# Per-head sums of squares and the spread of their scales: 32x32 turns on VectorE in place of PE transposes

## The reference

```python
y = concatenate([sb_out, fx_out, m_out])          # (1, 1024, 20 * 64)
yf = y.reshape(b, s, TOTAL_HEADS, HEAD_DIM)
yf = yf * rsqrt(mean(yf * yf, axis=-1) + EPS)     # per token and head, EPS = 1e-6
yf = yf.reshape(b, s, MIX_WIDTH) * out_norm_w
x = x + (yf * silu(gate)) @ w_out
return rmsnorm(x, final_norm_w)
```

## Time and profile before

| | |
|---|---|
| runs, device time | 803.50, 803.75, 803.94 us, median 803.75 |
| span of the profiled execution | 801.8 us |
| PE, DVE, ACT, POOL busy | 792.6, 580.4, 454.9, 239.2 us |
| share of the span | 99%, 72%, 57%, 30% |
| transfers | 88.9 MB, mean 111 GB/s |

### The profile page before, as it was taken

One profiled execution on the slowest core, in us unless ns is written; L12 is line 12 of the kernel. 1 busy time (PEld: TensorE's weight loads), 2 busy tenths in 40 slices (PEclk: granted clock), 3 DMA queues, 4 the chain that ended last, 5 costly groups with the idle time before them and its releaser, 6 DMA issues.

```text
span 801.8 us, 12113 instructions
## 1 busy us (share of the span) xinstructions
PE 792.6 (99%) x4184; PEld 671.3 (84%) x4184; DVE 580.4 (72%) x1178; ACT 454.9 (57%) x928; POOL 239.2 (30%) x378
## 2 busy tenths in 40 slices
PE   9999999999999999999999999999999999999997
PEld 8878888888888888888888888888888888888885
DVE  6877666676668887767788776779657677875575
ACT  7767665556647555665745576565546483542232
POOL 0112631342245225234533341454233111410000
PEclk9999999999999999999999999999999999999999
DMA  9414823114122411411061131104312298152532
GB/s 345 155 53 151 273 80 117 54 41 131 40 79 51 134 40 67 132 39 54 30 175 46 67 103 69 53 27 114 110 54 67 82 371 300 54 179 79 184 132 105
DMA packets 35276, 88.93 MB, mean 111 GB/s; under 512 B 3592, under 2 KB 11784, under 8 KB 34192
## 3 DMA queue, kind: packets, MB, share of 16 engines
q1 hardware_dynamic: 35216, 88.17, 33.3%
HBM read 57.72 MB, written 21.53 MB: 99 GB/s over the span
## 4 chain that ended last, share of the span: by engine, by line
PE 94%; DVE 2%; DMA 2%; issue 1%; ACT 1%; SPq 0%; ACTq 0%; DVEq 0%
PE banks L818 16%; PE banks L820 16%; PE banks L819 16%; PE banks L863 11%; PE banks L993 9%; PE banks L1013 5%; PE banks L980 5%; PE banks L1012 5%; PE banks L979 5%; PE banks L1064 1%; PE banks L950 1%; PE banks L945 1%; PE banks L1033 1%; DMA hT<-wo_dram 1%; PE banks L935 1%
## 5 line engine op out<-in xcount | busy, mean ns | idle before, releaser
L818 PE MATMUL banks<-hT,w_parts 128*128 128x512 f32 x576 | 237.3, 412 | 0.2 <-DVE sb_heads L1661 0.2
L820 PE MATMUL banks<-hT,w_parts 128*128 128x512 f32 x576 | 225.9, 392 | 0.0
L819 PE MATMUL banks<-hT,w_parts 128*128 128x512 f32 x576 | 225.4, 391 | 0.0
L1775 DVE TENSOR_TENSOR pT<-banks,pT 128x512 fp32r<-128x512 f32 x208 | 108.3, 563 | 88.9 <-ACT pT L1222 87.3
L1222 ACT ACTIVATE pT<-banks 128x512 fp32r<-128x512 f32 x208 | 92.5, 497 | 135.3 <-PE banks L993 135.1
L820 PEld LDWEIGHTS banks<-hT,w_parts 128*128 128x128 f32 x576 | 108.1, 188 | 24.5
L818 PEld LDWEIGHTS banks<-hT,w_parts 128*128 128x128 f32 x576 | 108.5, 188 | 15.0 <-DVE sb_heads L1661 0.7
L819 PEld LDWEIGHTS banks<-hT,w_parts 128*128 128x128 f32 x576 | 108.9, 189 | 13.3
L1490 POOL TENSOR_TENSOR w_parts<-w_raw,w_parts 128x1024 fp32r<-128x1024 f32 x34 | 81.5, 2398 | 95.9 <-ACT w_parts L1122 95.9
L1735 DVE TENSOR_TENSOR_SCAN work<-work 128x639 f32<-128x639 f32 (+3 forms) x64 | 90.6, 1416 | 4.7 <-POOL work L1497 4.6
L1198 ACT ACTIVATE work<-banks 128x512 f32<-128x512 f32 (+2 forms) x96 | 47.5, 495 | 71.0 <-PE banks L980 60.8
(11 more groups left out here) (248 smaller groups left out, 1366.3 us busy)
## 6 DMA issues: line engine op xcount, KB each, us to landing
w_raw<-in_w_tiles SPq DMA_DIRECT2D x36, 512.0 KB, 4.1
hT<-wo_dram SPq DMA_DIRECT2D x14, 512.0 KB, 8.0
fx_heads<-fx_heads SPq DMA_DIRECT2D x8, 512.0 KB, 7.5
negL<-negL_dram SPq DMA_DIRECT2D x8, 512.0 KB, 6.5
yT_dram<-silu SPq DMA_DIRECT2D x8, 512.0 KB, 5.1
sb_heads<-sb_heads SPq DMA_DIRECT2D x8, 512.0 KB, 7.0
negL<-yT_dram SPq DMA_DIRECT2D x8, 512.0 KB, 5.0
work<-in_x SPq DMA_DIRECT2D x6, 512.0 KB, 7.0
```

What stands on the lines that cost most here:

```text
L818: pe.matmul(o, w[0][:, k, :], hT[:, 0, k, tok], start=(k == 0), stop=False)
L819: pe.matmul(o, w[0][:, k, :], hT[:, 1, k, tok], start=False, stop=False)
L820: mm = pe.matmul(o, w[1][:, k, :], hT[:, 0, k, tok], start=False, stop=(k == KT - 1))
L1775: dve.tensor_tensor(pT[:, n % 3, 1, cols], banks[:, T_BANK + n % 2, cols], pT[:, n % 3, 0, cols].bitcast(F32), ALU.subtract).then_inc(t_lo, 1)
```

## The change

**N1.** ACT squares `yT` out of SBUF straight into the small bank, with the factor 1/64 in its scale. It is feature-major there, and DVE turns it in 32x32 blocks: within each block rows and columns change places, but the blocks stay where they are. Into `o_tmp` go 128 partitions x 512, in which partition 32 i + t holds token t of a 32-column block, and the 32 columns of a block are a quarter of the features of the pair. DVE sums 32 at a time to 16 numbers of a half. A head has two quarters, so its sum is that of two partition groups: at the second N1 of a phase DVE copies `head_sums` with neighbouring groups of 32 partitions swapped, in four copies, and adds. The scales are then 128x32 for a phase where they were 128x16, with each number there twice, and DVE's start, POOL's Newton steps and ACT's spread work on that shape.

**NT.** For the softmax heads EPS times the square of the row totals must come in the same layout. In the six phases behind such a pair POOL copies the totals four times side by side at tick 1 (`totals`), a new small piece NT at tick 2 transposes that with one PE transpose, and DVE turns it by 32x32 blocks and makes `head_eps` in two instructions.

**N3.** DVE turns the spread scales of one half from SBUF into the small bank, and goes on as before.

**Waits.** N1 and N3 are no longer in PE's row. ACT's square waits for `small_done` and `o_read`; DVE's N3 waits for `spread`. `o_tmp` is used twice now, so ACT's copy of an output waits for the N1 before it. ACT's sigmoids of a phase's first ticks wait for N3's `small_done`. SP's row is not changed.

```diff
@@ small_pieces @@
+            if c and PHASES[ph - 1][0] != "sb":
+                out.append(Small("NT", 0, ph - 1, UNITS * ph + TOTALS_TICK + 1))
@@ PE: small(n) @@
-                if n:
+                if n and p.what in ("VT", "MT", "NT"):
                     pe.wait_ge(small_done, n)
...
-                elif p.what == "N1":
-
-                    pe.wait_ge(o_read, 4 * p.of + 2 + TURN[p.c] + 1)
-                    for b in range(4):
-                        t = 4 * p.c + b
-                        mm = pe.transpose(o[:, b * P:(b + 1) * P], yT[:, t * P:(t + 1) * P], ident[:, :])
+                elif p.what == "NT":
+                    pe.wait_ge(totals_in, NT_BEFORE[n] + 1)
+                    mm = pe.transpose(o[:, 0:P], totals[:, :, :].rearrange("p i f -> p (i f)"), ident[:, :])
                 else:
-                    pe.wait_ge(spread, p.of + 1 + (TURN[p.c] if p.of == LAST else 0))
-                    for b in range(4):
-                        t = 4 * p.c + b
-                        mm = pe.transpose(o[:, b * P:(b + 1) * P], spread_of(p.of)[:, t * P:(t + 1) * P], ident[:, :])
+
+                    return
...
-            small(small_of("N3", 0, LAST))
@@ ACT: square_rows, spread_scales, output_lo @@
+                if g % 4 == 3:
+
+                    act.wait_ge(small_done, small_of("N1", 1, t.ph) + 1)
+                elif g % 4 == 0 and g:
+                    act.wait_ge(small_done, small_of("N1", 0, t.ph - 1) + 1)
...
-                act.wait_ge(small_ready, n + 1)
-                act.activation(banks[:, SMALL_BANK, :], banks[:, SMALL_BANK, :], ACT.Square).then_inc(sq_done, 1)
+                p = SMALL[n]
+                act.wait_ge(small_done, n)
+                act.wait_ge(o_read, 4 * p.of + 2 + TURN[p.c] + 1)
+                act.activation(banks[:, SMALL_BANK, :], yT[:, p.c * CW:(p.c + 1) * CW], ACT.Square, scale=HD ** -0.5).then_inc(sq_done, 1)
...
-               head3[:, 0, NB * c0:NB * c1].unsqueeze(2).broadcast_to((P, NB * (c1 - c0), HD)),
+               head3[:, 0, 2 * NB * c0:2 * NB * c1].unsqueeze(2).broadcast_to((P, 2 * NB * (c1 - c0), Q4)),
@@ POOL: spread_totals @@
+                row = rowsum[:, ph % 2, :, :].rearrange("p b h -> p (b h)")
+                pool.tensor_copy(totals[:, :, 0:2 * NB], row.unsqueeze(1).broadcast_to((P, P // Q4, 2 * NB))).then_inc(totals_in, 1)
@@ DVE: small pieces @@
+                elif p.what == "NT":
+
+                    dve.wait_ge(small_ready, READY_BEFORE[n] + 1)
+                    link(dve.transpose(totals[:, :, :].rearrange("p i f -> p (i f)"), src[:, 0:P]))
+                    for h in range(2):
+                        mine = slice(h * HD, (h + 1) * HD)
+                        z = totals[mine, :, h:2 * NB:2].rearrange("p a b -> p b a")
+                        ins = dve.scalar_tensor_tensor(out=head_eps[mine, :].rearrange("p (b a) -> p b a", b=NB), in0=z, scalar=EPS, in1=z,
+                                                       op0=ALU.mult, op1=ALU.mult)
+                    ins.then_inc(small_done, 1)
                 elif p.what == "N1":
...
-                    link(dve.reduce_sum(sums, src.rearrange("p (n d) -> p n d", d=HD), AX_X))
+                    link(dve.transpose(o_tmp[:, :], src))
+                    ins = dve.reduce_sum(head_sums[:, mine], o_tmp[:, :].rearrange("p (n d) -> p n d", d=Q4), AX_X)
...
+                    for i in range(P // Q4):
+                        ins = dve.tensor_copy(head_swap[i * Q4:(i + 1) * Q4, mine], head_sums[(i ^ 1) * Q4:(i ^ 1) * Q4 + Q4, mine])
+                    link(ins)
...
                 else:
-                    dve.wait_ge(small_ready, n + 1)
+                    dve.wait_ge(spread, p.of + 1 + (TURN[p.c] if p.of == LAST else 0))
+                    link(dve.transpose(src, spread_of(p.of)[:, cols]))
                     dve.wait_ge(gy_done, 2 * p.of + TURN[p.c] + 1)
```

51 lines of the change are left out of this document (37 added, 14 removed).

## The result

The changed kernel takes 822.72 us (median of four runs, 821.22 to 823.79), the kernel before 803.62: ratio 1.0236, 95% interval 1.0222 to 1.0251. Slower was the likelier side, but the time lies 11.7 us above the forecast of 811.0 and 2.7 above the end of the range.

The account below looks back on a forecast made before the run. PE, 99% busy, and DVE together bound the stick-breaking stretch. Memory -0.3, forgetting -1.6, stick-breaking +8.8 and +1.4, end -1.1 sum to +7.2 us on 803.75: 811.0 us, range 797 to 820.

Parts of the forecast that it names:

- The price of N1: DVE's turn, four copies and additions at a phase's second N1: 1.2 us later, 0.9 to 2.0.
- POOL: Three Newton steps on 128x32 instead of 128x16: 0.42 us longer, 0 to 0.7.
- The path: Stick-breaking phase: N1 with POOL +1.6, first N3 +0.72, holding PE at Q's evacuation +2.3 us; phase sum +2.9.
- the second N3: Stick-breaking phase, between the two evacuations: +0.72 less 0.25 slack, +0.5 us.
- The forgetting phases behind: Two forgetting phases following stick-breaking ones: +0.85 us each, +1.7 together.
- The second memory phase: Memory phase where DVE and ACT alternate closely: -0.3 us taken of its -1.65.
- The last phase and the end: Last stick-breaking phase +1.4 us; the end -1.1, four blocks and idle saved against one uncovered N1.
- The full gain: Rival: PE's waits at DVE move with PE and turns fit DVE's idle; 786.5 us, chance 0.12.
- the second: Rival: only the back-to-back stretch pays, copies and POOL's part fit waits, forgetting phases keep their gain; 800 us, chance 0.18.
- the dear turns: Rival: DVE turns cost two passes, 1.22 us each; 820.6 us, chance 0.12.
- the point of decision: Full-gain rival's threshold: 2.2 us of DVE work between 385 and 407; less is free, more is paid.
- The cheap ends: Turn 0.48, POOL +0, copies 0.08: stick-breaking phase 1.1 us less, forgetting one 0.9; total 804.7 us.

Follow-up runs that it names:

- d_split: Kernel before, none of the change, DVE given one idle 1.2 us reduction at each of the two N3 in three stick-breaking phases; 810.23 us.
- n3_turn: Kernel before with only N3's turns moved to DVE, N1 left on PE's transposes; 805.40 us, ratio 1.0026.
- n1_turn: Changed kernel with N3 put back on PE's transposes, N1 still turned by DVE; 814.92 us, ratio 1.0145.
- after_pool: Changed kernel with the second N1 at tick 6 and POOL's Newton steps in tick 7 behind its masks; 799.93 us, ratio 0.9962.
- best_b: after_pool with first forgetting phase's second N1 at tick 7, second N3 from tick 11 to 12, first memory pair's spread and N3 a tick earlier; 794.69 us.
- d_long: Kernel before, none of the change, DVE given three idle 1.22 us reductions at the first N3 of three stick-breaking phases; 820.28 us.
- d_warm: d_long with fourteen zero-weight matmuls on PE ahead of its wait in each of the three phases; 814.36 us.
- after_early: Changed kernel with the second N1 of a phase at tick 6 in place of 7; 816.99 us, ratio 1.0170.
- after_p8: Changed kernel, second N1 still at tick 7, POOL's Newton steps behind the masks of tick 8, spread and N3 one tick later; 814.72 us.

## Why the forecast was wrong

- *The bound.* Right. PE and DVE share it in the stick-breaking phases; PE's saved time was waited away at the evacuation of Q. d_split, with none of the change, shows that DVE's lateness there is paid nearly in full.
- *The price of a turn.* Right: 0.72 forecast, 0.71 to 0.72 measured. n3_turn measures the term of N3 by itself, +2.1.
- *The price of N1.* Too small. Four copies with their wait were taken as 0.4 to 0.5 us, because small operations without a wait between them seemed to overlap; in the trace of before it is a small operation and the scan behind it that overlap so (387.28 + 0.18 against 387.37). The copies take 0.173 us each and do not overlap: 0.76 with the wait. With it N1 is +1.57 and not 1.2.
- *POOL.* Too small as well, +0.59 in place of 0.42. The steady operations grew as forecast (0.22 to 0.25 for a product), 0.12 for each of the three Newton steps. The other 0.23 come at their start, beside DVE's product: the second operation took 0.80 in place of 0.23, the third 0.29 in place of 0.57.
- *The path.* 2.83 measured for 2.34, so 0.5 a phase by these two terms (+0.37 and +0.17, less 0.05 at N3).
- *The clock.* The largest single step that failed, a term put at nothing: I took PE's wait at the evacuation of Q as the whole cost. Behind it the granted clock was at half for 3.4 us, 1.55 us more in each of three phases in the profiled execution, 4.6 in all. No row of the kernel before could show it: its longest wait in the phases is 0.7 us. The 0.5 of the second N3 falls away against it, so 3.1 of the miss are its, and 2.5 came back in the median when the waits were filled. It is not the whole failure: the mis-sized terms of this list make the other 7.4.
- *The forgetting phases behind.* +1.4 each and not 0.85. Two waits stand there, for the low part (1.0) and for the logits (0.6), and the same two terms of N1 and POOL reach them.
- *The second memory phase* is +0.8 and not -0.3: DVE's N1 (PE waits 0.7 at 116.9), and the turn of N3 ahead of ACT's exponentials and the evacuation of Q (1.36 at 130.5; the profile names no releaser there, but n3_turn has 1.15 at this place and n1_turn no wait). My -0.3 had no row behind it but the remark that the two engines alternate. *The last phase and the end* are 2.2 dearer together: PE waits 2.1 us at 723.3 and 0.8 before it where +1.4 in all was taken. N1 with its copies seems to be paid twice, once for each half: without the copies these two parts are 2.4 us shorter.
- *The rivals.* The full gain fell, and so did the second (the forgetting phases behind lost, they did not keep their gain) and the dear turns: the time lies next to their 820.6 by chance, with turns of 0.72. That the waits could move with PE is what after_pool to best_b then brought about: the point of decision was the place, and the place could be changed.
- *The range.* The cheap ends were added up (804.7), the dear ones were not. By its own dear ends (N1 2.0, a turn 1.25, POOL 0.7) the three stick-breaking phases cost 6.4 us more and the two forgetting ones 3.2, which is 820.6 already, past the range's end at 820.

The misses are +2.0 for N1, POOL and the head of the three phases, +3.1 for the clock net of the second N3, +1.1 in the two forgetting phases behind them, +1.1 and +0.5 in the first two phases, +0.4 in forgetting phase 3 and +2.2 in the last phase and the end: together some 10.5, the distance from +7.2 to +17.7. The other 1.2 of the 11.7 us lie between the median of the change and its profiled execution.

## What to carry to other kernels

Work that moves from the busiest engine to one with idle time costs what its place costs: look for the last point before it at which the receiving engine waits, and the next point at which another engine waits for it, and put the work ahead of the first. Follow the queues of the helpers behind it too (here POOL's twelve small steps ahead of masks), since moving a piece moves all that is issued in its tick. And price a wait of TensorE of 2 us or more with what may come with it. In this case that was half the clock for 3.4 or 6.8 us, behind 8 of 15 waits of 2.1 to 2.6 us and 9 of 9 of 3.4 us and more.

## What the hardware showed

In the change the granted clock fell about 1 us after PE had started again (0.8, 1.0 and 1.2 us). That delay is not fixed: over all 17 cases it fell between 1.1 us before PE's start (d_long) and 1.5 us behind it (d_long too), and stayed down for 3.4 us, or for 6.8 in four of them. The same wait of 2.2 us brought it down in one phase and not in the next: 8 of 15 between 2.1 and 2.6 us. This may be a part of why executions scatter: 2.6 us between the four of the change, 0.5 between those of d_split. It isn't shown: in after_early and d_long the executions with the lower mean clock are the longer ones, in the change they are not in that order. Matmuls with a weight of zeros in the wait hold the clock (d_warm, 1.00 in the window above).

DVE and POOL hold each other up in these rows. In the change POOL's first step takes 1.07 us beside DVE's scan, which starts 0.17 before it and lasts 1.22, against 0.24 for the same step later; in after_p8 DVE's step of 0.18 takes 1.21 beside POOL's product, until that ends:

```profile
394.99 1.07 POOL L1557 TENSOR_TENSOR head<-head 128x32 f32<-128x32 f32 x1 [6.48 <-DVE head L1627]
396.15 0.80 POOL L1558 TENSOR_TENSOR head<-head 128x32 f32<-128x32 f32 x1
...
397.73 0.24 POOL L1557 TENSOR_TENSOR head<-head 128x32 f32<-128x32 f32 x1
```

The Trainium skill says so too, page "Trainium Architecture — The Big Picture", section "What this means for kernel authors": of the engines only DVE and GpSimd contend for a port of SBUF, and it is an exclusive lock. These rows agree with it: the step of 1.07 us and the one of 1.21 end within 0.03 us of the other engine's instruction.
